# The mixer's chunk steps: the second head of each pair of probabilities is normalised by VectorE, the first by GpSimd

## The reference

```
# attention: the probabilities of one head and one block of 128 queries
p = exp(scores - mx)
denom = p.sum(-1) (+ exp(sink - mx) for the sliding-window heads)
out = (p / denom) @ v
# delta rule: one chunk after the other
v_new = u_c - w_c @ state
o     = qd_c @ state + a_c @ v_new
state = state * exp(gl_c) + kd_c.T @ v_new
```

## Time and profile before

| what | value |
|---|---|
| median of 3 runs | 2229.83 us |
| lowest and highest | 2229.81 and 2232.19 us |
| span of the profiled execution | 2228.2 us |
| median less span | 1.6 us |
| PE busy | 2175.7 us, 98% of the span |
| DVE, ACT, POOL busy | 1073.0, 945.0, 1068.8 us |
| chunk steps, from `nv 1` to the first output sum | 1714.9 to 1774.1 us of the span |

### The profile page before, as it was taken

One profiled execution on the slowest core, in us unless ns is written; L12 is line 12 of the kernel. 1 busy time (PEld: TensorE's weight loads), 2 busy tenths in 40 slices (PEclk: granted clock), 3 DMA queues, 4 the chain that ended last, 5 costly groups with the idle time before them and its releaser, 6 DMA issues.

```text
span 2228.2 us, 33238 instructions
## 1 busy us (share of the span) xinstructions
PE 2175.7 (98%) x10952; PEld 1757.2 (79%) x10952; DVE 1073.0 (48%) x1486; ACT 945.0 (42%) x1639; POOL 1068.8 (48%) x787
## 2 busy tenths in 40 slices
PE   8999999999999999999999999999999988999996
PEld 6788888888888888777688778888778666888885
DVE  7842224444442272555525832337667538666412
ACT  4343334343433443444433344334545545444422
POOL 5654445545444444444355654444431534555553
PEclk9999999999999999999999999999999999999998
DMA  4232323323332322211032232333220022323333
GB/s 140 94 104 94 96 89 106 97 94 94 94 104 94 99 94 95 62 62 58 29 104 85 94 104 94 95 100 101 86 75 13 1 76 67 94 95 99 98 104 104
DMA packets 53791, 194.33 MB, mean 87 GB/s; under 512 B 6096, under 2 KB 6352, under 8 KB 53712
## 3 DMA queue, kind: packets, MB, share of 16 engines
q1 hardware_dynamic: 52704, 191.13, 27.0%
q10 hardware_dynamic: 1008, 2.14, 0.3%
HBM read 191.14 MB, written 2.10 MB: 87 GB/s over the span
## 4 chain that ended last, share of the span: by engine, by line
PE 58%; issue 24%; POOL 15%; DVE 1%; ACT 1%; POOLq 1%; ACTq 0%; DVEq 0%
PE proj L676 15%; PE proj L678 15%; PE proj L677 15%; POOL w_lo L605 14%; PE aux L818 2%; PE proj L843 2%; PE proj L772 1%; PE proj L774 1%; PE proj L773 1%; PE aux L821 1%; PE aux L829 1%; PE proj L941 1%; PE aux L941 1%; PE proj L1071 0%; PE proj L800 0%
## 5 line engine op out<-in xcount | busy, mean ns | idle before, releaser
L605 POOL TENSOR_TENSOR w_lo<-w_stage,w_hi 128x512 fp32r<-128x512 f32 x716 | 990.1, 1389 | 1000.4 <-ACT w_hi L1290 999.5
L1290 ACT ACTIVATE w_hi<-w_stage 128x512 fp32r<-128x512 f32 x716 | 442.2, 628 | 819.6 <-PE proj L678 747.4
L676 PE MATMUL proj<-xh,w_hi 128*128 128x512 f32 x1696 | 667.9, 394 | 1.9 <-POOL w_lo L605 1.9
L677 PE MATMUL proj<-xl,w_hi 128*128 128x512 f32 x1696 | 660.2, 389 | 0.0
L678 PE MATMUL proj<-xh,w_lo 128*128 128x512 f32 x1696 | 660.2, 389 | 0.0
L676 PEld LDWEIGHTS proj<-xh,w_hi 128*128 128x128 f32 x1696 | 318.3, 188 | 79.3 <-POOL w_lo L605 9.7
L677 PEld LDWEIGHTS proj<-xl,w_hi 128*128 128x128 f32 x1696 | 318.4, 188 | 67.0 <-issue 2.4
L678 PEld LDWEIGHTS proj<-xh,w_lo 128*128 128x128 f32 x1696 | 318.3, 188 | 67.0
L676 PE MATMUL proj<-act_h,w_hi 128*128 128x512 f32 (+1 forms) x840 | 327.1, 389 | 0.3 <-POOL w_lo L605 0.3
L677 PE MATMUL proj<-act_l,w_hi 128*128 128x512 f32 (+1 forms) x840 | 326.8, 389 | 0.0
L678 PE MATMUL proj<-act_h,w_lo 128*128 128x512 f32 (+1 forms) x840 | 326.8, 389 | 0.0
(11 more groups left out here) (338 smaller groups left out, 2297.1 us busy)
## 6 DMA issues: line engine op xcount, KB each, us to landing
w_stage<-stream SPq DMA_DIRECT2D x358, 512.0 KB, 3.5
out<-x_res SPq DMA_DIRECT2D x3, 512.0 KB, 2.6
x_res<-x SPq DMA_DIRECT2D x2, 512.0 KB, 8.1
consts_sb<-consts ACTq DMA_DIRECT2D x1, 640.0 KB, 4.0
x_res<-x ACTq DMA_DIRECT2D x1, 512.0 KB, 7.1
out<-x_res SPq DMA_DIRECT2D x2, 256.0 KB, 2.0
x_res<-x SPq DMA_DIRECT2D x1, 256.0 KB, 3.2
x_res<-x ACTq DMA_DIRECT2D x1, 256.0 KB, 4.8
```

The costliest lines, as they stand in the source:

```text
L605: pool.tensor_tensor(w_lo[:, at, :], w_stage[:, at, :], w_hi[:, at, :].bitcast(F32), ALU.subtract).then_inc(stage_free, 1)
L676: pe.matmul(o, w_hi[:, slot, cols], hi, start=(b == 0), stop=False)
L677: pe.matmul(o, w_hi[:, slot, cols], lo, start=False, stop=False)
L1290: act.activation(w_hi[:, u % RING, :], w_stage[:, u % RING, :], ACT.Copy).then_inc(hi_done, 1)
```

## The change

VectorE gets a new helper, `scale_second(k)`, which multiplies the second head's probabilities by the second reciprocal and raises a new semaphore, `second_scaled`. GpSimd keeps one instruction for each pair, the first head's. TensorE's transposes and ScalarE's exponentials of two pairs later (they write the same buffer of `probs`) now wait for both semaphores. For an even pair a (and pair 0) the new instruction stands between the reciprocal and `scaled_x`. For an odd pair it stands behind `vn c`, ahead of the maxima of the next two pairs. Pair 15 is as before.

```diff
+        second_scaled = sem("second_scaled")
...
                 pool.wait_ge(mix_dve, DVE_STEP["rs", k])
-                for t in range(2):
-                    ins = pool.tensor_scalar(probs[:, k % 3, t, 0:w], probs[:, k % 3, t, 0:w], soft[:, k % 2, 1, t:t + 1],
-                                             None, ALU.mult)
-                ins.then_inc(pair_scaled, 1)
+                pool.tensor_scalar(probs[:, k % 3, 0, 0:w], probs[:, k % 3, 0, 0:w], soft[:, k % 2, 1, 0:1],
+                                   None, ALU.mult).then_inc(pair_scaled, 1)
...
                     pe.wait_ge(pair_scaled, k + 1)
+                    pe.wait_ge(second_scaled, k + 1)
...
                         act.wait_ge(pair_scaled, k - 1)
+                        act.wait_ge(second_scaled, k - 1)
...
+                def scale_second(k):
+                    w = pair_of(k)[3]
+                    dve.tensor_scalar(probs[:, k % 3, 1, 0:w], probs[:, k % 3, 1, 0:w], soft[:, k % 2, 1, 1:2],
+                                      None, ALU.mult).then_inc(second_scaled, 1)
...
                 scale_of(0)
+                scale_second(0)
                 scaled_x(0)
                 for c in range(1, CHUNKS):
...
                     made(dve.tensor_tensor(blocks_of(vnew[r:r + CHUNK, :]), blocks_of(aux[r:r + CHUNK, 0, :]),
                                            vbeta[r:r + CHUNK, :, c // 2, :], ALU.add), ("vn", c))
+                    scale_second(a - 1)
                     maxima(a)
                     maxima(b)
                     if c < CHUNKS - 1:
                         update_state(c)
                     scale_of(a)
+                    scale_second(a)
                     scaled_x(c)
```

## The result

The changed kernel takes 2236.4 us (median of 20 runs, 2233.26 to 2238.92), the kernel before 2231.4 us (20 runs, 2229.49 to 2238.6). The ratio is 1.0020, with a 95% interval of 1.0013 to 1.0027: 2.9 to 6.0 us slower. The forecast was 2.3 us and no measurable change; the measured median lies above its range of 2229.4 to 2234.9. Of the 4.3 us between the forecast and this median, 1.6 are the base: the forecast was added to 2229.83, the median of three runs, and 20 runs of the same kernel gave 2231.4.

A forecast was written before the change was run, and what follows sets the result against it. The prediction took TensorE to bound the kernel, delayed through VectorE's maxima and ScalarE. Chunk-step terms 0.52 + 0.03 + 0.81 + 0.94 = 2.30 us raised 2229.83 to 2232.1 us, no measurable change; range 2229.4 to 2234.9.

The forecast's parts named there:

- rival 4: TensorE's granted clock dips again with longer idling: one more dip 2233.5 us, two more 2235; chance 0.17.
- step 2: Second chunk step: TensorE's wait before `t 2` goes, but `mx 4` is 1.03 us late; +0.03 us.
- steps 3, 5 and 7: Chunk steps where VectorE's undisturbed 256-wide scaling delays the chain through ScalarE that ends TensorE's idling; +0.27 us each.
- the 0.85 us: TensorE's wait before `t 2`, the only visible gain, claimed to be given back within its own chunk step.
- step 1: First chunk step: VectorE's scaling waits 0.25 us for GpSimd and works 0.27, all passed to TensorE; +0.52 us.
- Step 6: Sixth chunk step: VectorE's scaling of pair 11 waits out GpSimd's gate product, `mx 12` 1.44 us late; +0.94 us.
- the gate: GpSimd's 1.26 us product behind its scaling of pair 11, claimed to hold up VectorE's scaling until 1761.30.
- the 0.50 of slack: Slack of ScalarE and TensorE behind pair 11's scaling, claimed to absorb 0.41 us if the gate is not met.
- rival 1: Pair 11's scaling comes before the gate, so the 0.94 us goes: 2231.2 us; chance 0.20.
- variant of rival 1: GpSimd gets in ahead of `scaled_x`: `mx 4` 1.34 us late (+0.34), the gate follows pair 11's scaling; 2231.5 us.
- The signs: Expected profile marks: scaling counts, longer scalings of pairs 1, 3 and 11, TensorE's changed waits, later `mx 12` and first output sum.
- step 4: Fourth chunk step: `mx 8` 0.27 us late, absorbed by ScalarE's wait for TensorE; 0.

The follow-up runs named there:

- e16: Kernel before, with 22 unread TensorE products in the waits of the chunk steps and 15 in the long wait behind them: 2228.3 us, ratio 0.9982.
- e15: Changed kernel, with 25 unread TensorE products in the waits of the chunk steps and 15 in the long wait behind them: 2228.7 us, ratio 0.9987.
- e1: Changed kernel, but VectorE scales only the even pairs' second heads, GpSimd both heads of the odd pairs: 2231.7 us, ratio 0.9998.
- e2_odd: Changed kernel, but VectorE scales only the odd pairs' second heads, GpSimd both heads of the even pairs: 2241.5 us, ratio 1.0043.
- e14: Changed kernel with 6 unread TensorE products, only in the waits of chunk steps 1 and 2: 2237.4 us, ratio 1.0022.
- e5: Changed kernel with 25 unread TensorE products in the waits of the chunk steps: 2232.1 us, ratio 1.0001.
- e9: Changed kernel, with pairs 1 and 3 back on GpSimd and the other odd pairs scaled before VectorE's wait for the new values: 2231.3 us, ratio 1.0000.
- e12: Changed kernel with pairs 5, 7, 9, 11 and 13 given back to GpSimd, so only odd pairs 1 and 3 are scaled late: 2231.0 us, ratio 1.0007.
- e6: Kernel before, with 22 unread TensorE products in the waits of the chunk steps: 2231.7 us, ratio 0.9996.
- e7: Changed kernel with the odd pairs' second head scaled before VectorE's wait for the new values, not behind it: 2230.5 us, ratio 0.9999.
- e10: e9 with 20 unread TensorE products in the chunk steps and 15 in the long wait behind them: 2226.65 us, ratio 0.9984.

## Why the prediction was wrong

**What failed: the sum was made at one clock.** The lower clock stood as rival 4, priced at 1.4 us a dip, with a chance of 0.17 for mostly one more; it tied the falls to single long waits. That is the step that failed: the price of a fall was about right, their number was not. In the profiled execution the clock was below 1.00 in five steps more than before. Steps: 59.15 and 57.86 us before, without and with the clock held by fill; 64.04 and 58.79 after. The clock's share is 1.3 us before and 5.3 after, so 4.0 of the 4.9 us are the clock's and 0.9 the change's own. (The fill itself costs e16 about 0.2 us in step 2, 8.94 us against 8.73 without fill and also at 1.00; with that off it is 3.8 and 1.1.) The working priced each wait as if the work around it kept its length; here the work itself got longer. The base does not excuse the miss: taken from its own base the range went up to 5.1 us more, and the measured 5.0 (2.9 to 6.0) stands at that edge, but by the falls of the clock and not by the sum.

**The terms, from e15 less e16:**

| step | forecast | measured at clock 1.00 |
|---|---|---|
| 1 | +0.52 | +0.40 |
| 2 | +0.03 | -0.40 |
| 3, 5, 7 | +0.27 each | +0.28, +0.32, +0.32 |
| 4 | 0 | +0.01 |
| 6 | +0.94 | 0.00 |
| sum | +2.30 | +0.93 |

The chain from `vn` through the maxima to ScalarE and `pv` was right in its place, and in steps 3, 5 and 7 in its size. Step 2 was too dear: part of the 0.85 us is kept, 0.2 by e16's step 2 without the fill's cost, 0.3 in e1, where the maxima are not late.

**What the meetings cost.** The working let VectorE's scaling wait for the whole rest of GpSimd's instruction. It lost 0.2 us less than that rest each time. Pair 1: the rest was 0.25 us, the scaling took 0.05 more than the 0.35 undisturbed; pair 3: 0.36, and 0.17 more; pair 11 in e15: 0.28, and 0.07 more; pair 3 in e2_odd: 1.00, and 0.80 more; pair 15 before: 1.20, and 1.00 more. This is why step 1 costs 0.40 and not 0.52.

**Step 6: the gate was over, or nearly.** The premise was that GpSimd's head of an even pair waits for both the new scaling and `scaled_x`, from the row at 1748.20. It was wrong here: GpSimd's 256 columns at 1724.30 took 1.08 us, 0.16 more than alone, and `scaled_x`, which started behind it at 1724.51, took 0.97 us instead of 0.75. In the kernel before it was the other way round: `scaled_x` started first, by 0.06 us, and GpSimd's instruction was the one to lose.

```profile
1722.16 0.75 DVE L2196 SCALAR_TENSOR_TENSOR x_res<-x_res,params_sb,prod 128x512 f32<-128x512 f32 x1
1722.22 1.48 POOL L643 TENSOR_SCALAR probs<-probs,soft 128x256 f32<-128x256 f32 x1 [3.36 <-DVE soft L2177]
```

Now GpSimd got in, so pairs 10 and 11 and the gate were over sooner. In the changed kernel's own profile part of that distance comes from `nv 6`, slowed by the clock. In e15, at full clock, the gate still had 0.28 us to run when the scaling of pair 11 began (the rows below, DVE and POOL); it took 0.56 us, `mx 12` was 0.48 late (by `nv 6` in e15 and e16) and not 1.44, and the 0.50 of slack that rival 1 names took it up. So rival 1 had this term right in its outcome, 0, though the scaling did not come first.

```profile
1758.71 0.56 DVE L2195 TENSOR_SCALAR probs<-probs,soft 128x512 f32<-128x512 f32 x1
...
1757.72 1.27 POOL L648 TENSOR_TENSOR mixed<-mixed,zc 128x512 f32<-128x512 f32 x1
```

The prediction took its variant of rival 1 from the Trainium skill ("SBUF — State Buffer", "Who interferes with whom"): the first to issue holds the shared ports for the whole instruction and the other fully blocks, which the page says of VectorE's modes that use both port pairs. That the first to start loses little agrees with both orders above. The amount does not hold for `scaled_x`: a full block would have cost it 0.9 us, and it lost 0.22.

**The signs.** Right: 15 scalings on each side, the wait at `t 2` gone, scalings of pairs 5, 9 and 13 undisturbed. Wrong: the disturbed lengths of pairs 1, 3 and 11 (0.40, 0.52 and 0.48 us against 0.5, 0.6 and 1.5), and the waits of steps 3, 5, 6 and 7, which did not all grow. Counted from `nv 1`, `mx 12` started 4.7 us later and the first output sum 4.9, not 2.5 and 2.3; in e15 less e16 it is 1.1 and 0.9.

**What stays open.** That the loss runs through the clock is shown; why the clock fell where it did is not. It held through the steps in all eight kernels whose waits were filled throughout. But up to the end of step 2, e14 is the same program as e5, and there it fell to 0.83 in its profiled execution and e5 did not. e9 had less idle time than the kernel before and fell further in steps 3 and 4, and e12 did not fall there. The falls also differ from run to run: 123 of the 132 runs of the kernel before had a clock of 0.992 or more and nine had 0.989 or 0.990, and the fall near 1113 us is there in the profile of e5 and not in that of e15, which are the same program up to the long wait. So the number of a single profile's falls is partly luck. That the change costs about 1 us of its own rests on the profiles of the pairs e5 and e6, e15 and e16 (0.91 and 0.93 us, 0.2 more with the fill's cost taken off) and on few runs of equal clock (0.8 to 1.4 us). The intervals of e15 and e16 overlap, so by them alone it could be nothing.

## What to carry to other kernels

Where TensorE waits often for short times, price an edit at both levels of its clock: before the change it was already below full in two of seven steps, and some 0.3 us more on the chain that ends the waits cost 3 to 5 us here. Look at busy time for the same number of matmuls, step by step: when it grows and the idle time doesn't, no schedule of the other engines explains the loss. Compare runs at their granted clock as well: it told here in one table what the medians did not. Products that nobody reads, no longer than the wait that they fill, took the loss away, and with the long wait behind the steps filled too all three kernels were 3 to 4 us faster than before by the ratio; twice as many in the steps took it back. And an instruction that is moved to another engine did no harm ahead of that engine's wait (e7), and did behind it.

## What the runs showed of the hardware

- An unread product of 128 by 128 in fp32 shows as two matmuls and held TensorE for about 0.235 us: in e10 30 matmuls went into a wait of 3.8 us that left 0.3 of it.
- The same 66 matmuls of step 4 took 7.67 us at a granted clock of 1.00, 8.88 at 0.85 and 14.14 at 0.50: 1.00 is the 2.4 GHz level, 0.50 the 1.2 GHz level, 0.85 a mixture of both; twice the time at 1.00 would be 15.34.
- VectorE's instruction with two inputs from SBUF (`scaled_x`), beside GpSimd's scaling of 128, 256 and 384 columns, took 0.86, 0.97 and 1.07 us instead of 0.75: it lost about 0.11 us for each 128 columns, not GpSimd's whole time (0.69, 1.08 and 1.47 us).
- VectorE's scaling of `probs` beside a GpSimd instruction that had started first lost that instruction's rest less 0.2 us: 0.05, 0.07, 0.17, 0.80 and 1.00 us for rests of 0.25, 0.28, 0.36, 1.00 and 1.20.
- Two kernels with the same instructions on TensorE took the same time at the same mean granted clock: 2236.6 and 2236.5 us at 0.990, 2238.3 and 2238.5 at 0.989.
